# First block of a two-block transformer kernel: one phase for both layers, normalisation moved behind the projections, biases spread by transfers

## What is computed

```python
def hybrid_layer(x, ...):
    h = rms_norm(x, g_pre)
    a_q, a_kv, a_g, b_cq, b_ckv, b_kr, c_q, c_kv, z = split_cols(h @ w_in)
    o_a = nsa_attention(...)            # 4 heads, three branches each
    o_b = causal_block_attention(...)   # 4 heads, low-rank queries and keys
    o_c = banded_attention(...)         # 8 heads, window 128
    mixed = jnp.concatenate([o_a, o_b, o_c], axis=-1) * jax.nn.silu(z)
    return x + rms_norm(mixed @ w_out, g_post)
```

## Time and profile before

| | us |
|---|---|
| median of 3 runs (2660.51 to 2672.22) | 2661.77 |
| the profiled execution, its own time | 2659.23 |
| its span in the profile | 2657.4 |
| PE busy | 2513.5 (95%) |
| DVE busy | 1274.9 (48%) |
| ACT busy | 685.4 (26%) |
| POOL busy | 673.9 (25%) |

### The profile page before, as it was taken

How to read it: one execution, slowest core, us unless ns; L and a number is a source line. 1 busy time by engine, 2 the same in 40 slices (tenths; PEclk the granted TensorE clock), 3 DMA queues, 4 the chain that set the end, 5 groups by cost and what they waited for, 6 DMA issues and landing times. The chain is left out here.

```text
span 2657.4 us, 35733 instructions
## 1 busy us (share of the span) xinstructions
PE 2513.5 (95%) x13328; PEld 2002.8 (75%) x13328; DVE 1274.9 (48%) x1879; ACT 685.4 (26%) x1365; POOL 673.9 (25%) x516
## 2 busy tenths in 40 slices
PE   7999879998799999999899999899999999999997
PEld 4875558765488888787688888688887887788886
DVE  4446454465443334586733344433344876533344
ACT  2126431165221110354311110311100642311101
POOL 1006430064233321200433311233311101433311
PEclk9999989998899999998999999899999999999999
DMA  5310123200322332230233332233322321233322
GB/s 205 95 56 1 41 94 98 69 1 17 102 87 95 99 111 91 72 97 25 87 100 98 95 113 89 64 95 97 112 99 72 96 65 56 83 99 95 116 98 75
DMA packets 57556, 223.35 MB, mean 84 GB/s; under 512 B 6696, under 2 KB 7848, under 8 KB 57056
## 3 DMA queue, kind: packets, MB, share of 16 engines
q1 hardware_dynamic: 56000, 213.97, 25.0%
q10 hardware_dynamic: 1440, 7.79, 0.8%
HBM read 219.59 MB, written 2.15 MB: 83 GB/s over the span
## 5 line engine op out<-in xcount | busy, mean ns | idle before, releaser
L171 DVE CAST two_hi<-two_raw 128x1024 fp32r<-128x1024 f32 (+1 forms) x292 | 219.8, 753 | 907.6 <-PE bank L240 897.1
L233 PE MATMUL bank<-xh,two_hi 128*128 128x512 f32 x1728 | 429.8, 391 | 0.1
L240 PE MATMUL bank<-xl,two_hi 128*128 128x512 f32 x1728 | 427.5, 389 | 0.0
L236 PE MATMUL bank<-xh,two_lo 128*128 128x512 f32 x1728 | 426.8, 389 | 0.0
L173 DVE TENSOR_TENSOR two_lo<-two_raw,two_hi 128x1024 fp32r<-128x1024 f32 (+1 forms) x292 | 400.9, 1373 | 10.0
L236 PEld LDWEIGHTS bank<-xh,two_lo 128*128 128x128 f32 x1728 | 324.4, 188 | 67.6
L240 PEld LDWEIGHTS bank<-xl,two_hi 128*128 128x128 f32 x1728 | 324.4, 188 | 67.2
L233 PEld LDWEIGHTS bank<-xh,two_hi 128*128 128x128 f32 x1728 | 322.9, 188 | 68.6 <-issue 1.4
L1464 POOL TENSOR_TENSOR up_hm<-up_sg,up_hm 128x512 f32<-128x512 f32 x88 | 197.5, 2244 | 555.9 <-ACT up_hm L1446 555.9
L233 PE MATMUL bank<-hh,two_hi 128*128 128x512 f32 x704 | 171.8, 392 | 0.0
L240 PE MATMUL bank<-hl,two_hi 128*128 128x512 f32 x704 | 171.4, 390 | 0.0
(11 more groups left out here) (318 smaller groups left out, 3131.9 us busy)
## 6 DMA issues: line engine op xcount, KB each, us to landing
two_raw<-in_up SPq DMA_DIRECT2D x180, 512.0 KB, 3.5
two_raw<-in_down SPq DMA_DIRECT2D x64, 704.0 KB, 4.0
one_raw<-in_w_in SPq DMA_DIRECT2D x52, 512.0 KB, 3.6
two_raw<-in_w_in SPq DMA_DIRECT2D x40, 512.0 KB, 3.6
one_raw<-in_w_out SPq DMA_DIRECT2D x16, 512.0 KB, 3.5
two_raw<-in_w_out SPq DMA_DIRECT2D x16, 512.0 KB, 3.7
w<-in_w ACTq DMA_DIRECT2D x2, 2048.0 KB, 10.5
x<-in_x SPq DMA_DIRECT2D x1, 2048.0 KB, 8.3
```

The source lines that it names most:

```text
L171: v.tensor_copy(st.hi[:, h, 0:w], st.raw[:, r, 0:w]).then_inc(st.hi_made, 1)
L233: pe.matmul(out[:], st.hi[:, slot, k * P:(k + 1) * P], xh[:, h * kp + k, :], start=h == 0 and k == 0, stop=False)
L236: pe.matmul(out[:], st.lo[:, slot, k * P:(k + 1) * P], xh[:, h * kp + k, :], start=False, stop=False)
L240: mm = pe.matmul(out[:], st.hi[:, slot, k * P:(k + 1) * P], xl[:, h * kp + k, :], start=False, stop=h == pieces - 1 and k == kp - 1)
```

## The change

- Both layers are written out in one block, without a hardware loop or barriers between start, attention and output.
- x comes in four pieces, with the first weights between them. `xh` and `hn` are x times the gain alone (two ACT instructions for each row), not times 1/rms. The sum of squares is made meanwhile (seven additions on DVE, one matmul after tile 3), and 1/rms multiplies each tile of w_in at its eviction. Evictions are DVE's now; ACT applies Silu to the 8 z tiles in place. The first tiles use six banks.
- The bias rows by distance are made after the first two tiles. They are written to DRAM 128 times over from 4 and 8 partitions (`far`, `near`), and read back, shifted and already in order, straight into `biasA` and `biasC`. The turning matmuls and their copies go; `biasK` is read from `biasA` with a stride of 16.
- The first two tiles of w_out are split by DVE inside the attention, after pairs 17 and 20. ACT makes `xh` of the finished `mixed` rows from pair 44 on, POOL makes `xl` after its last scaling, and w_out takes the rows in the order in which they get ready (`TILES`).
- Output tiles 2 to 7 stay in PSUM; ACT squares them there, DVE scales them there and adds them to x. POOL adds no more. The next layer's `xh`, `hn` and first products follow each row of x as it is made. The squares of x after the last layer are gone, and so are four weight tiles that were fetched at the end and not used.

The core of the diff (new code; `...` marks what is left out):

```diff
+def rows_arriving(pe, st, n, banks, order, xh, xl, wait_hi, wait_lo):
+    ...
+    pe.wait_ge(st.w_split, n + 1 + RAW_RING)
+    for k in range(together):
+        wait_hi(k)
+        high(0, k)
+        if k == 0:
+            pe.wait_ge(st.w_split, n + 2 + RAW_RING)
+        high(1, k)
+        if k:
+            wait_lo(k - 1)
+            low(0, k - 1)
+            low(1, k - 1)
+    ...
+    def store_bias(sp):
+        sp.wait_ge(s["vec_made"], 3)
+        sp.dma_start(d["far"], first.vec[0:A_HEADS].unsqueeze(1).to_broadcast([A_HEADS, P, 2 * T])
+                     ).then_inc(s["stored"], 16)
+        sp.dma_start(d["near"], first.near[:].unsqueeze(1).to_broadcast([C_HEADS, P, NEAR_W])).then_inc(s["stored"], 16)
+    def read_bias(sp):
+        sp.wait_ge(s["stored"], 32)
+        for dst, name, sem, heads, w, n in ((kit.biasC, "near", "read_c", C_HEADS, NEAR_W, 256),
+                                            (kit.biasA, "far", "read_a", A_HEADS, 2 * T, BIAS_W)):
+            src = d[name]
+            sp.dma_start(dst[:], bass.AP(src.tensor, src.offset + P - 1, [[w - 1, P], [w * P, heads], [1, n]])
+                         ).then_inc(s[sem], 16)
+    ...
+    def sync(sp):
+        for n in range(max(n0, RAW_RING), n0 + st.per_layer):
+            sp.wait_ge(st.w_split, n + 1)
+            fetch_first(sp, st, n)
+            if n == 7:
+                begin["store_bias"](sp)
+            if n == 11:
+                begin["read_bias"](sp)
+    def scalar(a):
+        for c in range(DC):
+            if before:
+                a.wait_ge(before["x_made"], c + 1)
+            elif c % 2 == 0:
+                a.wait_ge(start[f"x_in{c // 2}"], 16)
+            gain = kit.gains[:, 0, l, c:c + 1]
+            a.activation(kit.xh[:, c, :], kit.x[:, c, :], ACT.Copy, scale=gain).then_inc(s["xhi_made"], 1)
+            a.activation(hn[:, c, :], kit.x[:, c, :], ACT.Copy, scale=gain).then_inc(s["hn_made"], 1)
+        for c in range(DC):
+            a.activation(xsq[:, c, :], kit.x[:, c, :], ACT.Square).then_inc(s["xsq_made"], 1)
+        a.dma_start(s1[:], d["s1"][l]).then_inc(s["s1_in"], 16)
+        a.dma_start(w1[:], d["w1"][l]).then_inc(s["w1_in"], 16)
+    ...
+        convert_at = {NU - 4: (0, 1), NU - 3: (2, 3), NU - 2: (4, 5), NU - 1: (6,)}
+    ...
+    def vector(v):
+        def evict(i):
+            v.wait_ge(st.mm_done, n0 + i + 1 + HL_RING)
+            if i == 0:
+                v.wait_ge(s["rstd_made"], 1)
+            ...
+            if i in SCALED:
+                out = v.scalar_tensor_tensor(proj[:, i, :], src, HD ** -0.5, kit.xrstd[:], ALU.mult, ALU.mult)
+            else:
+                out = v.tensor_tensor(proj[:, i, :], src, kit.xrstd[:], ALU.mult)
+        ...
+        for i in range(N_IN):
+            if i < N_IN - HL_RING:
+                split(i + HL_RING)
+            if i == 1:
+                if l == 0:
+                    begin["mask_rows"](v)
+                for c in range(1, DC):
+                    ...
+                    v.tensor_tensor(xsq[:, 0, :], xsq[:, 0, :], xsq[:, c, :], ALU.add).then_inc(s["xsq_added"], 1)
+            if i == 3:
+                for e in range(3):
+                    evict(e)
+            if i >= 3:
+                evict(i)
+            ...
+        v.wait_ge(start["read_c"], 16)
+        for j in range(NU + WEIGH_LAG + 1):
+            if j == N_SWA + N_MLA:
+                v.wait_ge(start["read_a"], 16)
+            step(j)
+            if j in SPLIT_AT:
+                split(N_IN + SPLIT_AT.index(j))
+    ...
+def project_out(kit, first, l):
+    def scalar(a):
+        for c in range(DC):
+            src = bank[Y_BANKS[c]]
+            ...
+            a.activation(sq[:, c % 2, :], src[:], ACT.Square).then_inc(s["sq_made"], 1)
+            if c < Y_KEPT:
+                a.activation(y[:, c, :], src[:], ACT.Copy).then_inc(s["y_kept"], 1)
+    def vector(v):
+        ...
+        for c in range(DC):
+            row = y[:, c, :] if c < Y_KEPT else bank[Y_BANKS[c]][:]
+            v.scalar_tensor_tensor(row, row, kit.gains[:, 1, l, c:c + 1], rs[:], ALU.mult, ALU.mult
+                                   ).then_inc(s["scaled"], 1)
+            v.wait_ge(s["scaled"], c + 1)
+            v.tensor_tensor(kit.x[:, c, :], row, kit.x[:, c, :], ALU.add).then_inc(s["x_made"], 1)
```

More of the change, by code:

```diff
@@ L80 @@
 UNROLL = 4
+BIAS_W, NEAR_W = 896, 384
 LINE = 64
@@ L442, in attention_pairs, with fetch_first @@
+def fetch_first(sp, st, n):
+    l, i = divmod(n, st.per_layer)
+    name = "w_in" if i < N_IN else "w_out"
+    src = st.dram[name]
+    at = l * st.n[name] + i - st.base[name]
+    u = n % RAW_RING
+    sp.dma_start(st.raw[:, u, :], src[at:at + 1].rearrange("o p k -> (o p) k")).then_inc(st.w_loaded[u], 16)
 def attention_pairs():
@@ new lines, in weight_tile @@
+def weight_tile(pe, st, n, out, order, xh, xl):
+    slot = n % HL_RING
+    pe.wait_ge(st.hi_made, n + 1)
+    for k in range(DC):
+        w = order[k]
+        pe.matmul(out[:], st.hi[:, slot, w * P:(w + 1) * P], xh[:, k, :], start=k == 0, stop=False)
+    pe.wait_ge(st.w_split, n + 1 + RAW_RING)
+    for k in range(DC):
+        w = order[k]
+        pe.matmul(out[:], st.lo[:, slot, w * P:(w + 1) * P], xh[:, k, :], start=False, stop=False)
+    for k in range(DC):
+        w = order[k]
+        mm = pe.matmul(out[:], st.hi[:, slot, w * P:(w + 1) * P], xl[:, k, :], start=False, stop=k == DC - 1)
+    mm.then_inc(st.mm_done, 1)
@@ L611, in _, with first_block @@
+def first_block(kit):
+    with ExitStack() as ctx:
+        first = First(kit, ctx)
+        begin = start_engines(kit, first)
+        layers = [(attend(kit, first, l, begin), project_out(kit, first, l)) for l in range(DEPTH)]
+        block = ctx.enter_context(kit.nc.Block())
         @block.sync
         def _(sp):
-            load_weights(sp, st, l, "w_in")
+            begin["sync"](sp)
+            for att, out in layers:
+                att["sync"](sp)
         @block.scalar
         def _(a):
-            w1_at = d["w1"][bass.ds(l, 1)].rearrange("o p k -> (o p) k")
@@ L867, in weigh @@
-            def weigh(x):
-                u = pairs[x]
-                tile = u["tile"]
-                out = bank[out_bank[tile]]
-                wait_copies(pe, groups_of[x][-1])
-                order = tiles_in_order.index(tile)
-                if order >= 2:
-                    pe.wait_ge(s["mixed"], order - 1)
-                for y in range(u["m"]):
-                    for hh in range(2):
-                        mm = pe.matmul(out[HD * hh:HD * hh + HD, u["n"] * P:(u["n"] + 1) * P],
-                                       values(u, hh, u["lo"] + y), pt(x)[0:u["rows"], hh, y * P:(y + 1) * P],
-                                       start=u["first"] and y == 0, stop=u["last"] and y == u["m"] - 1)
-                mm.then_inc(s["pv_mm"], 1)
@@ L1118, in phase_leave @@
+            for att, out in layers:
+                att["gpsimd"](g)
+                out["gpsimd"](g)
 def phase_leave(kit, tags):
     st = kit.stream
-    with kit.nc.Block() as block:
-        @block.sync
-        def _(sp):
-            wait_stream_end(sp, st)
     with kit.nc.Block() as block:
```

1268 lines of the change are left out of this document (625 added, 643 removed).

## The result

The changed kernel takes **2689.68 us** (median of 5 runs, 2687.95 to 2690.06), the kernel before 2661.77 (now 5 runs). The ratio taken over all these runs is 1.0092, with a 95% interval of 1.0078 to 1.0107; that of the two medians is 1.0105. It is slower by 28 us where 57 less were forecast, and above the range of 2588 to 2662. What came is the first rival, "The stores hold up the weights" (2687, chance 0.19). The profiled execution took 2688.14, its span is 2686.3; the one before had 2659.23.

What follows compares the result with a forecast made beforehand. PE was taken to run without gaps on weight tiles and to wait for rows at the turns between stages; gains and losses of 27.5 - 2.0 + 15.0 + 21.8 + 3.5 - 8.0 - 3.5 = 54.3 off 2659.2 gave 2605 us, range 2588 to 2662.

Steps and rivals of the forecast that it cites:

- the first rival: Tile 8 of layer 0: slow far and near stores delay the weights behind them; 2687 us, chance 0.19.
- the cost of the stores: Far and near stores ahead of weight tiles 8 to 11 in SP's queue: costed at 0, hidden by tiles 2 to 7.
- The forecast's lower case: Bias stores: one engine per source partition at 26 GB/s, far 20 us, near 7.5, tile 8's matmuls late by nothing or little.
- The upper bound: Bias stores: four partitions together at one engine's 26 GB/s, 110 us for both, 2605 + 82 = 2687.
- the deciding point: Time of both bias stores above which the change is slower: 82 us.
- Start: Beginning of layer 0: first product at 10.0 us, tile 2 (first without waiting for rows) at 28.2, 27.5 us earlier.
- The 14.7 us for the arriving tiles: Start of layer 0: the first two tiles, run as rows arrive, take 14.7 us as before, ending at 24.7.
- Attention to w_out: Turn from attention to w_out: tile 2 7.5 us earlier, 15.0 in both layers.
- the splits: Two w_out tile splits per layer inside the attention, behind pairs 17 and 20: 2 us each, 8 later for four.
- the conversions: ACT's w_out row conversions among the attention's last exponentials: 2 us of delay, between bounds of 0 and 3.7.
- Turn to layer 1: From the last w_out product to tile 2 of layer 1: DVE row pairs every 1.4 us, tile 2 21.8 us earlier.
- End of w_in: Last w_in tiles, both layers: DVE's evictions delay the last transposes by 1.25 and 0.5 us, 3.5 later in all.

Runs made afterwards that it cites:

- experiment 2: Experiment 1's kernel with far stored from four and near from eight partitions, each four partitions apart: 2607.99 us, one run.
- experiment 5: Experiment 1's kernel with the first two w_out splits on DVE behind the attention's last step instead of behind pairs 17 and 20: 2615.7 us.
- experiment 7: Experiment 1's kernel with ACT's eight conversions for w_out all behind the attention's last copy: 2596.06 us, ratio 0.9744 to the kernel before.
- experiment 6: Experiment 1's kernel with DVE's scaled rows written to an SBUF tile, so the addition to x reads two SBUF operands: 2608.62 us.
- experiment 8: Experiment 1's kernel with four copies of each bias row, and DVE's small chains ahead of the eviction at w_in's end: 2596.88 us.
- experiment 3: Experiment 1's kernel with far stored from partitions 32 apart and near from partitions 16 apart: 2640.3 us, one run.
- experiment 4: Changed kernel with the slow stores in ACT's queue, read back behind weight tile 24, DVE's wait for them at tile 20: 2614.48 us, one run.
- experiment 10: Changed kernel with far's four copies of each row stored from 16 partitions side by side, near as it was: 2628.8 us, one run.
- experiment 1: Changed kernel with the bias rows copied onto all 128 partitions and the same bytes stored from there: 2605.39 us, ratio 0.9787 to the kernel before.

## Why the prediction was wrong, point by point

**The step that failed** is the cost of the stores, which was put at 0, "hidden by tiles 2 to 7"; it measured 85.3, the gap of 83.5 and 1.8 behind it. It rests on two sentences: "The nearest row is the store of twelve rows of 4 KB: 113 GB/s at a share of 0.31 ... If one engine serves each source partition, at 26 GB/s, far takes 20 us and near 7.5." The value between the bounds was chosen by a row of 0.4 us, in which each partition gave one packet at most: it has eleven packets of 4 KB at 0.16 us each, and the trace doesn't tell the store's from the last of the weight tiles ahead of it, which have the same size. A steady stream from partitions side by side never occurred there. The forecast's lower case, one engine's rate for each row, is what experiment 2 gives with rows on four ports; the changed kernel has all four rows of `far` on one, and the first four of `near` with them: 2.10 and 0.79 MB in 114.5 us, 25 GB/s. The upper bound, 110 us for both and 82 late, was right to 5%: 114.5 and 83.5. Both ends, the place and the deciding point were there; what was wrong was the weight. The Trainium skill (SBUF — State Buffer, "Door 1: The DMA port swizzle") spoke against the change with a measured 27.6 GB/s for just these four partitions. The trace agrees, at 25. I gave the case 0.19 because a row of another kind seemed to speak against it. With that figure of the Trainium skill the prediction's own terms give about 2682, an estimate, and not the 2685 given there.

**The range**, meant for 8 chances in 10, left out the rival with its 0.19. With 0.4 or more on it, it would have had to reach to 2690.

**The other steps** were right in sum and partly in their parts. Start: first product at 9.67 (10.0), tile 2 1.7 late. The 14.7 us for the arriving tiles came from a start at which both were already split; here PE made two products and then waited 2.65 for tile 1's split, which DVE made beside POOL's `xl` in 3.9. The prediction had the two splits follow each other, but did not count the second. Attention to w_out: the first product follows the last weighting at once and tile 2 comes 12.1 behind it instead of 21.0. But the attention before it grew by 6.1 and 3.8 us; by experiments 5 and 7 the splits cost 2.3 and 3.2 of it (I took 4), the conversions 1.6 and 1.7 (I took 2), and unlike the splits the conversions are cheaper behind it. Turn to layer 1: pairs of 1.39 us, 22.2 earlier, and experiment 6 shows that the PSUM operand is what keeps them short. End of w_in: 2.05 a layer instead of 1.75, and experiment 8 takes it back. That the sum of these came out at 56.6 against 54.3 is in part luck, for errors of 1 to 4 us went both ways. Not foreseen: 3.5 in the second block.

## What to carry to other kernels

Before a transfer out of a few partitions goes on a path (only stores were tried here), divide its bytes by the groups of four neighbouring partitions that its rows reach, not by engines or rows: 25 to 27 GB/s for each group here, whatever the number of engines. Two rows 32 partitions apart counted as one group (experiment 3). If a matmul makes the rows, repeating its weight columns puts copies on all partitions at hardly any time of PE (four matmuls 1.98 us instead of 1.88), and took the stores from 114 us to within the 15 of that row (33 to 48). Ask as well what stands behind a slow transfer in its queue; and when an upper bound and a rule with a measured number point the same way, do not let a row that is short and of another kind outweigh them.

## What the runs showed of the hardware that I had not expected

- The DMA that was issued behind the slow store held its issuing engine: 34.2 us on SP in the changed kernel, 38.9 on ACT in experiment 4. It was 15.7 and 7.6 in experiments 3 and 2, where `far` moved at 52 and 108 GB/s, and 0.76 in experiment 10, where its 512 packets lay on sixteen engines. What waits there are instructions of the engine, not only transfers.
- DMA engines count as busy while such a group of four partitions holds them back: a share of 0.96 at 102 GB/s (experiment 8), where 1.03 was 418. The share alone does not tell how near the engines are to their rate.
- The second block is 3.5 us shorter in the changed kernel. It differs at one place: DVE's idle time ahead of the first row of its second layer, which ended by nothing that the profile shows, is 7.8 us in the kernel before and 3.5 to 3.8 in the changed kernel and all ten experiments. DVE's row of the kernel before, then of the changed one:

```profile
1689.04 1.54 DVE L1225 SCALAR_TENSOR_TENSOR x<-x,s,ln 128x256 f32<-128x256 f32 x3 [7.79 <-issue]
```

```profile
1717.39 1.54 DVE L1340 SCALAR_TENSOR_TENSOR x<-x,s,ln 128x256 f32<-128x256 f32 x3 [3.71 <-issue]
```

  Its cause was not tried.
- The granted clock fell for a while at different places of w_in in different kernels, with the same work there. From tile 2 of layer 1 to its first logits the changed kernel and experiment 7 took 146.7 and 146.8 us at a mean clock of 1.00, experiment 6 150.2 at 0.98, experiments 1 and 5 151.5 at 0.97 (experiment 1: 0.80 to 0.87 between 444 and 477 us). Why it fell in one and not in another was not tried. So a term of 2 to 5 us, read from single executions, is known only together with the clock of its stretch.
